# The first gate weight unit is split by GpSimd during attention instead of by ScalarE and VectorE after it

## The reference, cut to what matters

```
h = rms_norm(x); proj = h @ w_in
qa, ka, va, qb, kb, vb, ga, gb, mg = split(proj)
ya = banded_attention(qa, ka, va, 128, ..., sink) * silu(ga)
outs, lses = dilated_group(q_g, k_g, v_g) for three groups of 8 heads
yb = sum(softmax(lses) * outs) * silu(gb)
gates = sigmoid(mg + b_merge)
merged = gates[0] * (ya @ w_branch_a) + gates[1] * (yb @ w_branch_b)
out = x + merged @ w_out
```

## Time and profile before

| | |
|---|---|
| time, median of 3 runs | 1380.6 us (1380.26 to 1381.1) |
| time of the profiled execution | 1377.38 us |
| its span | 1375.4 us |
| PE busy | 1247.8 us (91%) |
| DVE busy | 550.8 us (40%) |
| ACT busy | 493.6 us (36%) |
| POOL busy | 174.7 us (13%) |
| mean granted clock of TensorE | 0.957 of full speed |

### The profile page before, as it was taken

The page is one execution under the profiler, slowest core; times in us unless marked ns, Lnnn a source line. Parts: engine busy times, 40 slices in busy tenths (PEclk is TensorE's granted clock), DMA queues, the critical chain, the costliest instruction groups (busy, mean ns, idle before and its releaser), DMA issues. The chain is left out here.

```text
span 1375.4 us, 24575 instructions
## 1 busy us (share of the span) xinstructions
PE 1247.8 (91%) x10411; PEld 976.0 (71%) x10411; DVE 550.8 (40%) x974; ACT 493.6 (36%) x860; POOL 174.7 (13%) x238
## 2 busy tenths in 40 slices
PE   5999999999989689988883799999999989989988
PEld 5787865799868455545441698888896668878888
DVE  3434553435372323322224513344438754453342
ACT  4234547512353311111012424455537654332230
POOL 4000013100010023221211001122200005300000
PEclk9999999999999889998897899999999999999999
DMA  4421000000229669999995445422207036212031
GB/s 154 130 92 62 31 1 0 10 5 4 64 89 358 234 240 389 392 385 388 401 391 210 98 141 137 106 92 89 79 17 116 40 103 205 61 62 92 1 107 47
DMA packets 92056, 193.44 MB, mean 141 GB/s; under 512 B 10102, under 2 KB 73676, under 8 KB 79020
## 3 DMA queue, kind: packets, MB, share of 16 engines
q1 hardware_dynamic: 86172, 181.38, 38.6%
q0 software_dynamic: 5200, 8.40, 1.9%
q10 hardware_dynamic: 576, 2.10, 0.4%
HBM read 183.69 MB, written 15.76 MB: 145 GB/s over the span
## 5 line engine op out<-in xcount | busy, mean ns | idle before, releaser
L1899 PE MATMUL hidden_ps<-w_gate,gathered_t 128*64 128x256 f32 x432 | 112.2, 419 | 18.4 <-DMA w_up<-exp_w_up_dram 16.9
L1899 PE MATMUL hidden_ps<-w_up,gathered_t 128*64 128x256 f32 x432 | 112.2, 419 | 0.0
L1899 PEld LDWEIGHTS hidden_ps<-w_gate,gathered_t 128*64 128x64 f32 x432 | 62.9, 151 | 54.9 <-issue 27.2
L648 DVE TENSOR_TENSOR w_in_low<-w_in_raw,w_in_high 128x2048 fp32r<-128x2048 f32 x20 | 45.8, 2292 | 116.4 <-ACT w_in_high L640 116.4
L600 PE MATMUL proj_ps<-block_in_high,w_in_low 128*128 128x512 f32 x232 | 90.6, 390 | 0.0
L600 PE MATMUL proj_ps<-block_in_low,w_in_high 128*128 128x512 f32 x232 | 90.6, 390 | 0.0
L600 PE MATMUL proj_ps<-block_in_high,w_in_high 128*128 128x512 f32 x232 | 90.5, 390 | 0.0
L2732 PE MATMUL gate_ps<-block_in_high,gate_w_high 128*128 128x512 f32 x192 | 76.6, 399 | 5.2 <-DVE gate_w_low L648 5.2
L1461 PE MATMUL wo_ps<-w_out_high,wo_x_high 128*128 128x256 f32 x256 | 74.8, 292 | 3.5 <-DVE w_out_low L659 3.5
L2732 PE MATMUL gate_ps<-block_in_low,gate_w_high 128*128 128x512 f32 x192 | 75.3, 392 | 0.0
L2732 PE MATMUL gate_ps<-block_in_high,gate_w_low 128*128 128x512 f32 x192 | 75.3, 392 | 0.0
(11 more groups left out here) (470 smaller groups left out, 3129.7 us busy)
## 6 DMA issues: line engine op xcount, KB each, us to landing
w_gate<-exp_w_gate_dram SPq DMA_DIRECT2D x27, 1024.0 KB
w_up<-exp_w_up_dram SPq DMA_DIRECT2D x27, 1024.0 KB
w_down<-exp_w_down_dram SPq DMA_DIRECT2D x27, 1024.0 KB
w_in_raw<-w_in_dram SPq DMA_DIRECT2D x20, 1024.0 KB, 5.6
slot_scratch_and_keys<-w_in_dram SPq DMA_DIRECT2D x14, 1024.0 KB, 5.3
vb<-w_in_dram SPq DMA_DIRECT2D x6, 1024.0 KB, 5.7
gate_w_raw_odd<-w_in_dram SPq DMA_DIRECT2D x6, 1024.0 KB, 6.0
slot_scratch_and_keys<-exp_w_gate_dram SPq DMA_DIRECT2D x5, 1024.0 KB
```

What stands on the lines that cost most here:

```text
L648: dve.tensor_tensor(self.part[1][n % 2], self.slot(n), self.part[0][n % 2], ALU.subtract).then_inc(self.low, 1)
L1899: x = pe.matmul(g_bank[e % 2][a * CAP:(a + 1) * CAP, 0:DE], xT[e % 2][:, k, :], w[:, k, :], start=(k == 0), stop=(k == KC - 1))
```

## The change

GpSimd gets a list of its own in the attention block. It waits until DVE has added the last local bias, then until the first gate unit is loaded, makes the high part by a copy and the low part by a subtraction. The high part lies where `band1` was, the low part where the keys of the local group were. In the gate block, ACT and DVE no longer split unit 0, and PE reads unit 0 from the new places. As these places are used again in the gate block, the loads of the two branch weights now stand behind a wait for the first two tiles, and two turns later in SP's list; GpSimd's `widen` waits for the same two tiles.

```diff
     def parts(self, n, k, cols):
+        if n == 0 and self.first_part is not None:
+            return [p[:, k, cols] for p in self.first_part]
         return [p[n % 2][:, k, cols] for p in self.part]
+
+    def split_first(self, pool, parts):
+        self.first_part = parts
+        pool.wait_ge(self.loaded[0], 16)
+        pool.tensor_copy(parts[0], self.slot(0)).then_inc(self.high, 1)
+        pool.wait_ge(self.high, 1)
+        pool.tensor_tensor(parts[1], self.slot(0), parts[0], ALU.subtract).then_inc(self.low, 1)
...
+            @block.gpsimd
+            def _(pool):
+                pool.wait_ge(biased, HU * units.index((2, 0, 0)))
+                next_w.split_first(pool, T["gate_w_first"])
+
...
                     if n == NU - 2:
                         sp.wait_ge(joined, FT)
                         next_w.load(sp, 0)
-                    if n < 2:
-                        sp.dma_start(bw[n][:, :, :], (wa, wb)[n]).then_inc(b_in, 16)
+                    if n in (2, 3):
+                        sp.wait_ge(ready, 2)
+                        sp.dma_start(bw[n - 2][:, :, :], (wa, wb)[n - 2]).then_inc(b_in, 16)
...
             @block.scalar
             def _(act):
-                wts.split_high(act, 0)
                 for f in range(2 * NGU):
...
             def _(pool):
                 pool.wait_ge(groups.st, groups.STEPS)
+                pool.wait_ge(ready, 2)
                 for n in range(NWIDE):
...
             @block.vector
             def _(dve):
-                wts.split_low(dve, 0)
                 for f in range(2 * FT):
...
+            with Scope(nc) as below:
+                T["gate_w_first"] = [below.sb("gate_w_high0", [P, KC, UNIT], F32R)[:, :, :], const["gate_w_low0"][:, :, :]]
             T["band1"] = s.sb("band_bias", [P, NH, 2 * P])
...
             const["branch_high"] = [below.sb_right("branch_t_high1", [P, 2, S], F32R)]
+            below.sb_right("keys_behind_gate_w", [P, 3 * KC * DE - 2 * S - KC * UNIT])
+            const["gate_w_low0"] = below.sb_right("gate_w_low0", [P, KC, UNIT], F32R)
```

More of the change, by code:

```diff
@@ L612, in __init__ @@
         self.raw = [raw[:, i] for i in range(2)] if not isinstance(raw, list) else raw
-        self.tag, self.part = tag, None
+        self.tag, self.part, self.first_part = tag, None, None
         self.first, self.first_in = first, first_in
```

## The result

The kernel after takes 1371.38 us in the median of 20 runs (1364.15 to 1380.27), against 1380.43 us for 20 runs of the kernel before (1377.07 to 1385.18). The ratio is 0.9938 with an interval of 0.9922 to 0.9954: faster by 9 us, with 6 to 11 inside the interval (the experiments show that this interval is too narrow).

A forecast was written before the change was run, and what follows sets the result against it. PE, busy 91% of the span, was taken as the bound. Removed splits 4.27 us plus slow stretch 1.65 less unit 1's wait 0.4 gave 5.5 us off the 1380.6 us median: 1375.1 us, range 1372.8 to 1377.4.

The forecast's parts named there:

- the slow stretch: First eight gate matmul spacings, at half clock after the stall: at full clock with the change, 1.65 us gained.
- unit 1's wait: Gate block, after unit 0: the second gate unit lands 6.7 us after issue, so PE waits 0.4 us.
- one more unknown: Half-speed stretches after the two later stalls: length does not follow the stall, each may come out 1.0 us cheaper or dearer.
- The removed splits: Start of the gate block: PE no longer waits for ACT's and DVE's splits of unit 0, worth 4.27 us.
- rival (a): Gates' start: clock falls after the short stall too, as at 185.40; gain 4.27 us, 1376.3 us; chance 0.25.
- GpSimd: Third attention group: copy and subtraction take at most 10.4 us, hidden by attention; nothing added to the path through DVE.
- Rival (d): Third attention group: GpSimd keeps DVE out, some 8 us land on PE, 1383 us; chance 0.03.
- The queue: SP's list, branch loads moved back: unit 3 lands at most 15.3 us after issue, still hidden by 1.3 us.
- The sum: Whole change: 4.27 + 1.65 - 0.4 = 5.5 us, taken off the median of 1380.6 us, giving 1375.1 us.

## Why the prediction missed, step by step

In short: the place gave what was forecast, within 0.6 us. The two terms behind that, the slow stretch (1.65 us) and unit 1's wait (0.4 us), were off by 0.2 and 0.4 us. The step that put the time outside the range is the one that named "one more unknown": it allowed for chance only 1.0 us behind each of two stalls, where the runs show several microseconds over the whole kernel.

**The removed splits** were sized right: 4.27 us forecast, and PE's start moved from 4.32 to 0.05 us behind the first issue, 4.27 us.

**The slow stretch** was mis-sized. I took "1.65 us" from one profile. That the clock would hold behind a stall of 0.97 us was right, and rival (a) did not occur: in all eight profiles with that stall the clock stayed at 1.00. But the row that spoke for (a), 185.40, was not the rule at its own place either: behind that 0.94 us stall the clock fell in five of thirteen profiles. What the change saves is seen from PE's first gate matmul to its first with unit 1, which in the kernel before is

```profile
1143.23 0.39 PE L2732 MATMUL gate_ps<-block_in_high,gate_w_high 128*128 128x512 f32 x1
```

and so 12.55 us behind 1130.68. In the other four profiles with the stall of 5.24 us it is 13.78, 13.81, 12.51 and 12.98 us, in the three of the kernel after 11.27, 11.27 and 11.25. So to be rid of the stretch is worth 1.2 to 2.6 us, 1.9 in the mean. The clock alone would give more: by the 6.5 us windows the five profiles lost 1.6, 3.0, 3.0, 1.6 and 2.1 us, 2.3 in the mean, but the slower pace of unit 0 from its new places takes 0.3 of it back, which the prediction did not have. I had written that the length of such a stretch does not follow the stall, and used that for the two later stalls, not for the one that the change removes.

The Trainium skill (TensorE: Matmul & The Clock Gate, What's actually happening) says that the number of slow matmuls at a kernel's start differs from run to run for the same kernel. Here that holds for a stall within the kernel too, as the five losses above, 1.6 to 3.0 us, show.

**Unit 1** was taken at a wait of 0.4 us; it is 0. The load landed in 5.9 us and not 6.7, and PE came 0.4 us later than by 10.9 us, so unit 1 is ready 0.7 us ahead of PE. The mechanism was right: with 10.7 us to landing PE waits 4.49 us and the gain is gone.

**GpSimd** took 1.89 and 4.55 us where I had allowed 5.2 each, hidden either way; the forecast of nothing for DVE held. The rule of the Trainium skill (GPSIMD Engine Reference, Key points), that the two engines contend where VectorE has two SBUF inputs or a two-port mode, agrees for these forms, which have at most one: 422 and 686 ns with GpSimd beside them, 422 and 687 ns in the same forms over the whole third group. Rival (d) also had a slip in its sum: over 27 us DVE has 7 us of slack at 2.7 in each ten, not 2.7, so that DVE alone would have put 4 us on PE and not 8. With the block held by GpSimd until 1132, 5.7 us later, the rival comes to some 1381 us, no slower than the kernel before.

**The queue**: unit 3 landed 10.7 us after its issue, inside the bound of 15.3, and nobody waited for it.

**The sum** with the sizes that the runs showed is 4.27 + 1.9 - 0 = 6.1 us. The time to the first branch product agrees: 81.31, 82.55, 82.58, 81.27 and 81.75 us with the stall (mean 81.9), 75.78, 75.78 and 75.75 in the kernel after, 6.1 us less. In the very profile on which the prediction rests it is 5.5 us, the forecast sum; that is luck in part, since there the stretch gave 1.3 and not 1.65, and the missing wait made up for it. Off the median of 1380.6 the 6.1 us would have been 1374.5 us, inside the range. The tails differ by 6.6 us (248.9 and 242.3 in the mean), but 0.5 of that lies behind the first branch product, where the change moves nothing on PE's path.

**The rest of the 9 us**, about 3 us, is where the range failed. It counted the stretches behind two stalls, 1 us each. From the first branch product to the end, profiles of the same kernel after took 167.15, 167.88 and 164.61 us, 3.3 us between the highest and the lowest; behind the 0.94 us stall far ahead some 1.7 us are lost or not; single runs of the kernel after go from 1364 to 1380 us; and an unchanged kernel missed its own median by 5 us. A mean of 7.5 +- 1.4 us over all runs contains 6.1. The gate block's first issue, up to which only GpSimd's hidden work is new, came at 1124.0 to 1137.3 us (mean 1129.3) in the six profiles in which the early parts are not made or not read, and at 1124.4 to 1133.8 (mean 1127.8) in the six in which GpSimd's parts are used. That the excess of the first comparison is such scatter is argued from these numbers; no run shows it directly, and 1 or 2 us of true gain elsewhere would not be seen.

## What to carry to other kernels

When two splits or casts stand between a barrier and the first matmul, move them to engines that have idle time in the stage before (here idle GpSimd cost the attention nothing, and ACT and DVE 0.8 us), and look at once at what is next in the queue: here the gain exists only because the second unit's load moved to the front of it. A stall of PE costs its length and a part that is drawn anew in each run; take that part as a span over several profiles, not as one number. And before explaining an odd microsecond of a median, run the unchanged kernel against itself.

## What was unexpected of the hardware

Behind one and the same stall of 3.5 us before the output projection, three executions of one kernel had granted clocks of 0.77, 0.55 and 1.00 in the next 6.5 us. Behind 5.24 us it was 0.54 to 0.75. The stall of 0.97 us at the gates lowered it in none of eight profiles, but one of 0.94 us elsewhere did in five of thirteen. So a short stall is not safe by its length alone; what makes the difference between the two places is not shown. And unneeded matmuls in a stall, which cost nothing because PE had nothing else to do, kept it at 2.4 GHz in each of the three profiles that have them; before the output projection that is weak evidence, as one profile without them kept it too.

At full clock, matmuls of one form stood 0.233 us apart with weights read from one pair of places and 0.227 with weights from another, while the weight loads themselves took 0.188 us in both. The cause is open.
